# Mixers of a two-block transformer kernel: position bias accumulated in PSUM by TensorE, and four VectorE steps given to ScalarE

## What is computed

```python
def hybrid_layer(x, ...):
    u = rms_norm(x, attn_norm_w) @ w_in
    hq, hf, hi, hg, aq, ak, av, sz, sxbc, sdt = jnp.split(u, points, axis=-1)
    mix = jnp.concatenate([hgrn2_mixer(...), dilated_attention_mixer(...), mamba2_mixer(...)], axis=-1)
    x = x + (mix @ w_out)
    return x + peer_ffn(rms_norm(x, ffn_norm_w), ...)

def dilated_attention_mixer(q, k, v, q_norm_w, k_norm_w, rel_bias):      # 6 heads of 64
    q = rms_norm(q.reshape(bsz, seq, H, Dh), q_norm_w) * (Dh ** -0.5)
    k = rms_norm(k.reshape(bsz, seq, H, Dh), k_norm_w)
    ...
    s = jnp.einsum('bghnid,bghnjd->bghnij', qb, kw) + bias[None, None, :, None]
    s = jnp.where(mask, s, -jnp.inf)          # then softmax over keys, times v
...
# mamba2_mixer: a causal convolution of 4 taps over time, per channel
    xbc = conv(xbc, conv_w) + conv_b          # then silu
```

## Time and profile before

| | before |
|---|---|
| median of 3 runs (lowest to highest) | 2966.87 us (2962.67 to 2971.38) |
| the profiled execution, its span | 2973.62 us, 2971.8 us |
| granted TensorE clock over the span | 0.99 |
| TensorE busy | 2924.6 us (98%) |
| VectorE busy | 2022.1 us (68%) |
| ScalarE busy | 1456.4 us (49%) |
| GpSimd busy | 16.7 us (1%) |

### The profile page before, as it was taken

How to read it: one execution, slowest core, us unless ns; L and a number is a source line. 1 busy time by engine, 2 the same in 40 slices (tenths; PEclk the granted TensorE clock), 3 DMA queues, 4 the chain that set the end, 5 groups by cost and what they waited for, 6 DMA issues and landing times.

```text
span 2971.8 us, 43765 instructions
## 1 busy us (share of the span) xinstructions
PE 2924.6 (98%) x17198; PEld 2587.8 (87%) x17198; DVE 2022.1 (68%) x3133; ACT 1456.4 (49%) x2275; POOL 16.7 (1%) x40
## 2 busy tenths in 40 slices
PE   8999999999999999999999999999999999999998
PEld 7888888889999888888888999997898998888997
DVE  6859998765555685889885655567666556665554
ACT  6531775554444553257545444445455444545443
POOL 0000000000000000000000000000000000000000
PEclk9899999999999998999999999999999999999999
DMA  6334456774554433444668555556555656554563
GB/s 193 98 129 156 157 178 204 250 273 173 196 196 172 159 103 107 156 156 170 203 225 294 184 196 184 183 184 180 179 171 176 185 188 183 173 180 146 150 186 135
DMA packets 223293, 528.50 MB, mean 178 GB/s; under 512 B 13498, under 2 KB 87392, under 8 KB 212128
## 3 DMA queue, kind: packets, MB, share of 16 engines
q1 hardware_dynamic: 221872, 521.11, 52.9%
q0 software_dynamic: 1264, 5.25, 0.5%
HBM read 507.42 MB, written 18.88 MB: 177 GB/s over the span
## 4 chain that ended last, share of the span: by engine, by line
PE 92%; DVE 6%; ACT 1%; DMA 1%; issue 1%; SPq 0%; DVEq 0%; ACTq 0%
PE ps L2357 15%; PE ps L1275 15%; PE ps L2341 12%; PE ps L1325 12%; PE ps L1335 12%; PE ps L1309 11%; PE ps L559 3%; PE ps L568 2%; PE ps L1264 2%; PE ps L2601 1%; DVE ring_lo L542 1%; PE ps L692 1%; DVE arena L1626 1%; PE ps L1086 1%; PE ps L2524 0%
## 5 line engine op out<-in xcount | busy, mean ns | idle before, releaser
L1995 DVE TENSOR_TENSOR ring_lo<-ring,w_hi 128x1024 fp32r<-128x1024 f32 x320 | 388.7, 1224 | 264.6 <-ACT w_hi L1991 263.2
L1991 ACT ACTIVATE w_hi<-ring 128x1024 fp32r<-128x1024 f32 x320 | 336.4, 1056 | 263.5 <-PE ps L2357 178.5
L1275 PE MATMUL ps<-h_t,ring 128*128 128x256 f32 x2048 | 463.5, 379 | 0.9 <-ACT arena L908 0.9
L1275 PEld LDWEIGHTS ps<-h_t,ring 128*128 128x128 f32 x2048 | 379.2, 190 | 47.4 <-issue 1.3
L1325 PE MATMUL ps<-h_t_lo,down_hi 128*128 128x256 f32 x1024 | 288.3, 282 | 0.0
L1325 PE MATMUL ps<-h_t_expert,down_lo 128*128 128x256 f32 x1024 | 288.0, 281 | 0.0
L1325 PE MATMUL ps<-h_t_expert,down_hi 128*128 128x256 f32 x1024 | 286.9, 280 | 0.0
L2341 PE MATMUL ps<-h_t_hi,w_hi 128*128 128x256 f32 x928 | 260.2, 280 | 2.8 <-ACT arena L2147 2.7
L2341 PE MATMUL ps<-h_t_lo,w_hi 128*128 128x256 f32 x928 | 261.6, 282 | 0.0
L2341 PE MATMUL ps<-h_t_hi,ring_lo 128*128 128x256 f32 x928 | 259.8, 280 | 0.0
L1788 DVE TENSOR_TENSOR up_lo<-ring,up_hi 128x2048 fp32r<-128x2048 f32 x64 | 146.7, 2292 | 98.9 <-ACT up_hi L971 98.9
(11 more groups left out here) (463 smaller groups left out, 6682.2 us busy)
## 6 DMA issues: line engine op xcount, KB each, us to landing
ring<-in_peer_down SPq DMA_DIRECT2D x128, 1024.0 KB, 5.1
ring<-in_w_in SPq DMA_DIRECT2D x140, 512.0 KB, 3.7
ring<-in_peer_up SPq DMA_DIRECT2D x68, 1024.0 KB, 4.8
ring<-in_w SPq DMA_DIRECT2D x132, 512.0 KB, 3.7
ring<-in_peer_up SPq DMA_DIRECT2D x120, 512.0 KB, 4.2
arena<-late_gates SPq DMA_DIRECT2D x16, 1024.0 KB, 6.8
ring<-in_w_out SPq DMA_DIRECT2D x16, 512.0 KB, 3.6
ring<-in_peer_w_query SPq DMA_DIRECT2D x16, 512.0 KB, 4.3
```

The source lines that it names most:

```text
L1275: m = pe.e.matmul(PS[:, act_bank(b), j * T:(j + 1) * T], RING[:, b % 2, j * D + kc * P:j * D + (kc + 1) * P], HT[:, kc, :], start=kc == 0, ...
L1991: a.e.activation(W_HI[:, g % HI_SLOTS, :], RAW[:, g % RAW_SLOTS, :], ACT.Copy).then_inc(*a.count(f"c{g}_hi"))
L1995: v.e.tensor_tensor(RAW_LO[:, g % RAW_SLOTS, :], RAW[:, g % RAW_SLOTS, :], W_HI[:, g % HI_SLOTS, :].bitcast(F32), ALU.subtract).then_inc(* ...
```

## The change

TensorE no longer flips the bias at the front. It adds `FLIP` by `HANK` to each head's score in PSUM, right behind the product of queries and keys, and VectorE's evictions of the scores add `PHASE` only. `BIAS0` and `BIAS1` and their six evictions are gone. Four things that VectorE made are now ScalarE's: the squares of queries and keys (into a region of their own, `QKSQ`), the copy and the squares of the HGRN heads' output, the scaled queries and keys (the scale of the queries is made once per layer by a small VectorE operation), and the first tap of the convolution.

```diff
+        QKSQ = score_at + AT_HEADS * (T + P)
+        QKSQ = ARENA[:, QKSQ:QKSQ + 1536]
...
@@ hybrid_scalar
             front_high(a, (4, 2), (4, 3))
             tokens_out(3)
+            a.e.wait_ge(*a.mine())
+            a.e.activation(QKSQ.rearrange("p (t n) -> p t n", t=TT), U[:, :, 256:1024], ACT.Square).then_inc(*a.count("qk_sq"))
             front_high(a, (5, 0), (5, 1))
...
             a.e.activation(STAT[:, 88:112], STAT[:, 64:88], ACT.Sqrt).then_inc(*a.count("qk_sd"))
+            a.e.wait_ge(*a.at("hg_out"))
+            a.e.activation(SCORE[:, 0:512], PS[:, 4, :], ACT.Copy).then_inc(*a.count())
+            a.e.activation(SCORE[:, 512:1024], PS[:, 4, :], ACT.Square).then_inc(*a.count("hg_read"))
+            a.e.wait_ge(*a.at("q_scale"))
+            a.e.wait_ge(*a.at("qk_t"))
+            for c0, c1, w in ((0, 2, STAT[:, 57:58]), (2, 3, STAT[:, 57:58]), (3, 4, hpar("k_norm")), (4, 6, hpar("k_norm"))):
+                a.e.activation(QKT[:, c0:c1, :].rearrange("p c t -> p (c t)"),
+                               PS[:, 5 + c0 // 2, (c0 % 2) * T:(c0 % 2) * T + (c1 - c0) * T], ACT.Copy, scale=w) \
+                    .then_inc(*a.count("qkt" if c1 == 6 else None))
             front_high(a, (5, 2), (5, 3))
...
             front_high(a, (6, 0), (6, 1), (6, 2), (6, 3))
+            def taps(first, last, ready):
+                a.e.wait_ge(*a.at(ready))
+                for c in range(first, last):
+                    a.e.activation(XC[:, c, :], XB[:, c, 0:T], ACT.Copy, scale=hpar("conv_w", c, c + 1)) \
+                        .then_inc(*a.count(f"tap{c}"))
+            taps(0, 4, "h4_ev")
             a.e.wait_ge(*a.at("at_max"))
...
+            taps(4, CONV_TILES, "h5_ev")
             a.e.wait_ge(*a.at("dt_neg"))
@@ hybrid_tensor
-            pe.e.wait_ge(*pe.at(f"root@in{l}"))
-            pe.e.wait_ge(*pe.at("hank_in"))
-            for h in range(AT_HEADS):
-                m = pe.e.matmul(PS[:, 4 + h // 2, (h % 2) * T:(h % 2 + 1) * T], FLIP, HANK[:, h, :], start=True,
-                                stop=True)
-            m.then_inc(*pe.count("flip"))
...
-            pe.e.wait_ge(*pe.at("bias_ev"))
+            pe.e.wait_ge(*pe.at(f"root@in{l}"))
             pe.e.wait_ge(*pe.at("w128"))
...
+            pe.e.wait_ge(*pe.at("hank_in"))
             for h, q, k in heads():
-                m = pe.e.matmul(PS[:, 4 + 2 * (h % 2) + h // 4, (h // 2 % 2) * T:(h // 2 % 2 + 1) * T], q[:, P:T], k,
-                                start=True, stop=True)
+                to = PS[:, 4 + 2 * (h % 2) + h // 4, (h // 2 % 2) * T:(h // 2 % 2 + 1) * T]
+                pe.e.matmul(to, q[:, P:T], k, start=True, stop=False)
+                m = pe.e.matmul(to, FLIP, HANK[:, h, :], start=False, stop=True)
             m.then_inc(*pe.count("at_scores1"))
...
             for h, q, k in heads():
-                m = pe.e.matmul(PS[:, 4 + 2 * (h % 2), (h // 2) * P:(h // 2 + 1) * P], q[:, 0:P], k[:, 0:P], start=True,
-                                stop=True)
+                to = PS[:, 4 + 2 * (h % 2), (h // 2) * P:(h // 2 + 1) * P]
+                pe.e.matmul(to, q[:, 0:P], k[:, 0:P], start=True, stop=False)
+                m = pe.e.matmul(to, FLIP, HANK[:, h, P:T], start=False, stop=True)
             m.then_inc(*pe.count("at_scores0"))
@@ hybrid_vector
             v.e.memset(XB[:, :, 0:3], 0.0).then_inc(*v.count("hybrid_start"))
+            v.e.tensor_scalar(STAT[:, 57:58], hpar("q_norm"), HEAD ** -0.5, None, ALU.mult).then_inc(*v.count("q_scale"))
...
             v.e.wait_ge(*v.at("phase_in"))
-            v.e.wait_ge(*v.at("flip"))
-            for b in range(3):
-                v.e.tensor_tensor(BIAS1[:, 2 * b:2 * b + 2, :], ...
-                v.e.tensor_tensor(BIAS0[:, 2 * b:2 * b + 2, :], ...
             v.e.wait_ge(*v.at("decay64"))
...
-            v.e.tensor_tensor(sq, U[:, :, 256:1024], U[:, :, 256:1024], ALU.mult).then_inc(*v.count())
+            v.e.wait_ge(*v.at("qk_sq"))
+            v.e.tensor_reduce(STAT[:, 64:88], QKSQ.rearrange("p (n d) -> p n d", d=HEAD), AX.X, ALU.add).then_inc(*v.count())
...
-            v.e.wait_ge(*v.at("hg_out"))
-            v.e.tensor_copy(o, PS[:, 4, :]).then_inc(*v.count("hg_read"))
-            v.e.tensor_tensor(sq, o, o, ALU.mult).then_inc(*v.count())
-            v.e.wait_ge(*v.at("qk_t"))
-            for c0, c1, w in ((0, 2, "q_norm"), (2, 3, "q_norm"), (3, 4, "k_norm"), (4, 6, "k_norm")):
-                v.e.tensor_scalar(QKT[:, c0:c1, :]..., PS[:, 5 + c0 // 2, ...], hpar(w), ...
             front_low(v, (5, 1))
             v.e.wait_ge(*v.mine())
+            v.e.wait_ge(*v.at("hg_read"))
...
-                                  BIAS1[:, odd:4:2, :], ALU.add).then_inc(*v.count())
+                                  PHASE[:, 0:T].unsqueeze(1).broadcast_to([P, 2, T]), ALU.add).then_inc(*v.count())
...
-                                  BIAS0[:, odd:6:2, :], ALU.add).then_inc(*v.count())
+                                  PHASE[:, T:T + P].unsqueeze(1).broadcast_to([P, 3, P]), ALU.add).then_inc(*v.count())
...
-                    if k == 0:
-                        i = v.e.tensor_scalar(XC[:, c, :], XB[:, c, 0:T], w, None, ALU.mult)
+                    if k == 1:
+                        v.e.wait_ge(*v.at(f"tap{c}"))
...
-            conv(0)
             front_low(v, (6, 2))
             conv(1)
```

More of the change, by code:

```diff
@@ L430, in build @@
         QKT = split(QKT, "p (c t) -> p c t", c=6)
-        SCORE1, BIAS1 = (split(a[:, 0:AT_HEADS * T], "p (h s) -> p h s", h=AT_HEADS) for a in (SCORE, BIAS))
-        SCORE0, BIAS0 = (split(a[:, AT_HEADS * T:], "p (h s) -> p h s", h=AT_HEADS) for a in (SCORE, BIAS))
+        SCORE1 = split(SCORE[:, 0:AT_HEADS * T], "p (h s) -> p h s", h=AT_HEADS)
+        SCORE0 = split(SCORE[:, AT_HEADS * T:], "p (h s) -> p h s", h=AT_HEADS)
         DEC = split(SCORE, "p (h s) -> p h s", h=SS_HEADS)
@@ L1497, in hybrid_vector @@
             v.e.wait_ge(*v.at("phase_in"))
-            v.e.wait_ge(*v.at("flip"))
-            for b in range(3):
-                v.e.tensor_tensor(BIAS1[:, 2 * b:2 * b + 2, :],
-                                  PS[:, 4 + b, :].rearrange("p (h s) -> p h s", h=2),
-                                  PHASE[:, 0:T].unsqueeze(1).broadcast_to([P, 2, T]), ALU.add).then_inc(*v.count())
-                v.e.tensor_tensor(BIAS0[:, 2 * b:2 * b + 2, :],
-                                  PS[:, 4 + b, :].rearrange("p (h s) -> p h s", h=2)[:, :, P:T],
-                                  PHASE[:, T:T + P].unsqueeze(1).broadcast_to([P, 2, P]), ALU.add) \
-                    .then_inc(*v.count("bias_ev" if b == 2 else None))
             v.e.wait_ge(*v.at("decay64"))
@@ L1545, in hybrid_vector @@
             v.e.wait_ge(*v.mine())
-            sq = SCORE[:, 0:1536].rearrange("p (t n) -> p t n", t=TT)
-            v.e.tensor_tensor(sq, U[:, :, 256:1024], U[:, :, 256:1024], ALU.mult).then_inc(*v.count())
-            v.e.wait_ge(*v.mine())
-            v.e.tensor_reduce(STAT[:, 64:88], SCORE[:, 0:1536].rearrange("p (n d) -> p n d", d=HEAD), AX.X,
-                              ALU.add).then_inc(*v.count())
+            v.e.wait_ge(*v.at("qk_sq"))
+            v.e.tensor_reduce(STAT[:, 64:88], QKSQ.rearrange("p (n d) -> p n d", d=HEAD), AX.X, ALU.add).then_inc(*v.count())
             rstd("qk", 24, HEAD, 64, 88)
@@ L1557, in hybrid_vector @@
             front_low(v, (5, 0))
-            v.e.wait_ge(*v.at("hg_out"))
             o, sq = SCORE[:, 0:512], SCORE[:, 512:1024]
-            v.e.tensor_copy(o, PS[:, 4, :]).then_inc(*v.count("hg_read"))
-            v.e.wait_ge(*v.mine())
-            v.e.tensor_tensor(sq, o, o, ALU.mult).then_inc(*v.count())
-            v.e.wait_ge(*v.at("qk_t"))
-            for c0, c1, w in ((0, 2, "q_norm"), (2, 3, "q_norm"), (3, 4, "k_norm"), (4, 6, "k_norm")):
-                v.e.tensor_scalar(QKT[:, c0:c1, :].rearrange("p c t -> p (c t)"),
-                                  PS[:, 5 + c0 // 2, (c0 % 2) * T:(c0 % 2) * T + (c1 - c0) * T],
-                                  hpar(w), HEAD ** -0.5 if w == "q_norm" else 1.0, ALU.mult, ALU.mult) \
-                    .then_inc(*v.count("qkt" if c1 == 6 else None))
             front_low(v, (5, 1))
             v.e.wait_ge(*v.mine())
+            v.e.wait_ge(*v.at("hg_read"))
             v.e.tensor_reduce(STAT[:, 112:120], sq.rearrange("p (n v) -> p n v", v=HEAD), AX.X, ALU.add) \
```

4 lines of the change are left out of this document (2 added, 2 removed).

## The result

| | before | changed |
|---|---|---|
| median on one chip, 16 runs each (lowest to highest) | 2973.05 us (2962.67 to 2976.58) | 2978.98 us (2974.61 to 2984.41) |
| the profiled execution, its span | 2973.62 us, 2971.8 us | 2984.26 us, 2982.4 us |

The ratio is 1.0027, with a 95% interval of 1.0017 to 1.0037: the change costs some 8 us (0.0027 x 2973; 5 to 11 by the interval; the two medians differ by 5.9). A gain is excluded. The forecast was no change, 2967 us with a range of 2957 to 2977. The median lies 2 us above that range.

The account below looks back on a forecast made before the run. TensorE bounds the kernel with 92% of the chain, so only its work or waits count. Per layer -2.63 - 0.44 + 4.85 - 1.84 = -0.06 us, twice -0.1: 2967 us against the median 2966.87, range 2957 to 2977.

Parts of the forecast that it names:

- Scores with the bias (loss 4.9 us): Mixers' two score sets: 64-row products at full price alternating with FLIP products, plus 3.32 and 1.53, together 4.85 us per layer.
- The bound of 7.3: Upper bound for the scores per layer: 4.85 us plus 2.4 if each of 24 half/full array changes costs 0.1 us.
- The 0.1 us: Possible cost per half/full array change, read from the product following L1155 later than usual; could also be the block change.
- Bias flip at the front: Mixers' front: removing six FLIP matmuls and VectorE's evictions starts L1102 2.63 us earlier per layer, with about 1.7 us wait left.
- Squares: Squares of queries and keys move to ScalarE; the 0.44 us wait at the transposes L1141 goes whole, per layer.
- Scaled queries and keys: With the heads' output, moved to ScalarE before the scores: gain 0, scaled keys ready 4 us before TensorE asks.
- First tap: Convolution tap leaves VectorE: the tail comes 1.84 us earlier per layer, the dt-transposes wait goes, new waits of 1.4 to 1.6.
- Sum: All steps: -0.06 us per layer, -0.1 us for two layers; median 2967 us, with 0.68 given to the forecast.
- rival 1: Mixers' tail: the clock returns to 2.4 GHz, up to 6.8 us per layer back, 2953 us, or 2960 in one layer; chance 0.17.
- the clock (0.13): Mixers' tail: new waits keep the clock low through the attention output, plus 6.7 us per layer, 2980 us; chance 0.13.
- a late ScalarE (0.02): ScalarE late by 4 us at the scaled keys or dt's logarithm; to count, 4.5 us per layer, 2976 us; chance 0.02.
- alternating products of over 6 us: Sign that the forecast is wrong, at the scores: alternating products expected at 4.8 and 2.4 us take over 6.

Follow-up runs that it names:

- e1: Changed kernel with six score products first, then six FLIP products, in each set; part of the sum is left out: 2963.82 us, 0.9981 of the kernel before.
- e2: Changed kernel with each FLIP product one head later, still alternating but never adding onto the region just written: 2975.91 us, single run.
- e3: Changed kernel with FLIP products contracting over 64 rows only, leaving out half of the bias, still accumulating directly: 2962.98 us, single run.
- e4: Kernel before with only the four moves to ScalarE, bias flipped and added as before: 2962.59 us, ratio 0.9984.
- e5: Kernel before with the bias change alone, score and FLIP products alternating, nothing moved to ScalarE: 2983.81 us, ratio 1.0055.
- e7: Kernel before with the four ScalarE moves and the FLIP products placed once in TensorE's wait before the W128 products, evicted later: 2958.66 us, ratio 0.9964.
- e8: Kernel before with the moves to ScalarE except the first tap, which stays on VectorE: 2967.79 us, ratio 0.9997.
- e6: Changed kernel with score products grouped before FLIP products and start flags only at each PSUM bank's first product: 2965.02 us, 0.9986 of the kernel before.

## Why the prediction was wrong

**The step that failed is "Scores with the bias (loss 4.9 us)".** It priced a 64-row product that loses its partner at 0.40 us and a FLIP product at 0.40. Both fit: FLIP products take 0.42 among themselves in e1, and 0.40 + 0.22 is the 0.63 of a lone 64-row product, which no run has without a change beside it. It priced the 24 changes between half and full array at nothing, and gave them 0.1 us only for the upper bound. Measured, a change costs 0.22 us: 11 in each set, 22 per layer, 4.8 us, which is what 9.71 has over 4.85. The bound of 7.3 was too low by 2.4 us as well. The 0.1 us came from the product behind L1155, 0.22 us to the next against 0.12; that product is of another kind than the scores and the flips, and a change between two of those stood nowhere in the trace before. The row was no measure of the switch: behind the transposes L1141, which use 128 rows, the second product also comes 0.21 us after the first (83.61 to 83.82). The queue of weight loads did show the switch in the trace before, which the step did not look at. Behind L1155 (64 rows) and behind L1068 (128 rows):

```profile
90.94 0.19 PEld L559 LDWEIGHTS ps<-h_t_hi,out_lo 128*128 128x128 f32 x1 [0.33 <-issue]
```

```profile
35.77 0.19 PEld L568 LDWEIGHTS ps<-out_lo,h_t_hi 128*128 128x128 f32 x1
```

The load stands still for the same 0.33 us as between the products of the changed kernel's first set, and not at all where the height stays. The step chose nothing over 0.1 because the row could also be read as a change of block. A row with two readings deserved its 0.05 to 0.1 in the sum, and an upper bound well over itself; the scores would then have been plus 6 to 7 per layer and the whole plus 2 to 5 us, still short of what came, but on the right side. The Trainium skill (TensorEngine Tiling (Array Packing), "Key Properties") says that changing the tiling mode, unlike changing the tile, drains TensorE. The runs here agree with it (0.22 us for each change in the changed kernel and in e2, and none between two halves of one height in e3). It gives no figure. The prediction weighed that page's speedup and not this rule, which spoke for a price above nothing.

That the time left the stated range is in part the doing of its starting point: 6 to 8 us on top of 2966.87 would have been inside it, and so would 2978.98 in a range of the same width around 2973.05. A range of 10 us to each side covered a step that was wrong by 9.7 us in all. The rows of the scores show the error whatever the medians do.

Point by point:

- **Bias flip at the front, -2.63**: right in size, with VectorE setting it and a wait of 1.92 us left (forecast 1.7). In layer 0 the clock took 1.6 us of it back, below; in layer 1 the step gave 1.8 us, and the wait was 2.54 us where it had been 1.78. VectorE's chain to it began 7.48 us late (1014.35 to 1021.83) where TensorE was 6.70 late, behind a ScalarE that had waited 2.59 us for a weight transfer (0.67 before).
- **Squares, -0.44**: right; the wait is gone in the changed kernel and in e4, and stays in e5.
- **Scaled queries and keys, 0**: right. ScalarE's four evictions start at 82.51 and end by 84.5, 3.5 us before TensorE asks.
- **First tap, -1.84**: measured 8.33 - 6.71 = 1.62 in layer 0 and 14.04 - 12.37 = 1.67 in layer 1. The forecast said that the whole tail would move by it, with new waits; at L1238 the shift is +6.66, so it holds.
- **Sum**: with 9.71 in the forecast's own account, 2 x (9.71 - 2.63 - 0.44 - 1.84) = +9.6 us; the profiles differ by 10.6. That they come so close is in part luck. At the end of layer 1's mixers the lag is 12.37: 1.6 us of the clock, 0.2 of a late start in layer 0 and 0.8 of the shorter front gain in layer 1 stand on top of the 9.6 (12.2 in all), and 1.8 us come back behind the mixers. The medians differ less; what the clock may have to do with that stands with the result.
- **Rivals**: in the changed kernel the clock did not come back (0.77 over the shifted tail as before). It did elsewhere: over 130:160, which is not quite the same work in each, it is 0.75 to 0.77 before, in the changed kernel and in e7, 0.83 to 0.85 in e1, e4 and e5, 0.94 in e2, e3 and e8, and 1.00 in e6. e8 still has the wait of 1.6 us that rival 1 wanted gone, so that wait is not what decides it; what does stays open. Nor did the clock fall through the attention output: 125:130 is at 0.82, yet L1238 waits for VectorE all the same, so that stretch had slack. ScalarE was nowhere late for TensorE at the scores or at dt's logarithm. The slower side, 0.15, was given to the clock (0.13) and a late ScalarE (0.02); the mechanism that came had been left inside the forecast's bounds. Of the signs named as wrong, "alternating products of over 6 us" is the one that came.

## What to carry to other kernels

A product that uses fewer rows of the array than its neighbours costs a switch on each side, 0.22 us here, so group products by height and never alternate them: the same 24 products cost 12.1 us alternating and 6.3 grouped. An operation that is moved into another stage takes on the neighbours of that stage: price every change that it makes there. The queue of weight loads can show a price that the products' rows hide, as the 0.33 us behind L1155 did before the change; where no row shows it, put it in the sum and not only in the bound. Before merging work to save an eviction, look for a wait that could hide it where it is; here 2.4 us of products nearly fitted into a wait of 1.9 us, and that had the lowest ratio of all versions (0.9964; e4, which leaves the flips where they were, has 0.9984, and the two intervals just overlap).

## What the runs showed of the hardware

- **Switching heights.** 0.63 us per fp32 product of 256 columns when 64-row and 128-row products alternate, against 0.40; 0.42 against 0.20 with 128 columns. The extra does not grow with the columns. Two 64-row products in opposite halves share 0.43 us when others of 64 rows surround them, also where every second one accumulates (e3), and 0.63 us between two switches (e2).
- **Each half keeps its own order.** With 64-row products only, the product for the other half is recorded ahead of one that stands before it in the program (e3, four records of L1173 from 87.53 on, then four of L1174).
- **Start flags.** In PSUM the start flag of one product clears the marks of the whole bank: with several heads in a bank, six starting products followed by six adding ones do not add everywhere (e1), and starting only at each bank's first product does (e6). The Trainium skill (PSUM — Partial Sum Buffer, "The four PSUM rules") says so of the 2 KiB bank; it costs no time either way.
- **A fall of the clock that comes with the flip's place.** Over 41:48 the granted clock of layer 0 is, in one profiled execution of each, 0.76 in all six kernels without FLIP products ahead of the W128 wait (the changed one, e1, e2, e3, e5, e6) and 1.00 in all four that have them there (before, e4, e7, e8). Right before it TensorE stands still for 1.9 us in all of them but e7. Three of them, the last columns as above (e4, e5, e7):

```profile
41.00:48.00 7.00, 5.07 (x46) 3.80 (x46) 6.93 (x20) 5.77 (x9) 0.00 (x0) 1.00 0.38 116
```

```profile
41.00:48.00 7.00, 6.59 (x50) 5.20 (x52) 7.00 (x16) 6.25 (x11) 0.00 (x0) 0.76 0.24 83
```

```profile
41.00:48.00 7.00, 7.00 (x60) 5.32 (x60) 7.00 (x15) 5.57 (x9) 0.00 (x0) 1.00 0.31 93
```

So the wait alone does not decide the fall. In layer 1, over 1020:1040, the six are at 0.91 to 0.95 and e4, e7 and e8 at 1.00, but the kernel before at 0.91 as well, so the split isn't clean there. What decides it was not tried, and stays open; it took 1.6 of the 2.6 us that the flip's going had won in layer 0.
